# Layer 1's convolution stage as Strassen pairs on 128-token halves, with half of the weight sums on GpSimd

## The chip, the cores and the metric

The kernel runs on one core of a Trainium2 chip. The time is the device time of one execution in microseconds, the median of several runs; lower is better. Tiles have 128 partitions. The engines are TensorE (PE in the profile; its weight loads are PEld), VectorE (DVE), ScalarE (ACT), GpSimd (POOL) and SyncE (SP), which here only issues the weight transfers.

## The reference

Two transformer blocks in sequence, all in fp32, width 1024, on 256 tokens. The second has two layers and works on 256 context tokens beside the 256 latent ones. In its layer 0 both are carried through; in layer 1, the last, only the latent ones need the mixer's output. What matters here is the part of that mixer that the kernel calls the convolution stage:

```python
def _conv_module(glu, p):
    a, g = jnp.split(glu, 2, axis=-1)
    y = a * jax.nn.sigmoid(g)
    y = depthwise_conv_over_tokens(y, p['conv_w_dw'], width=31, pad=15) + p['conv_b_dw']
    y = silu(layernorm(y, p['conv_ln_g'], p['conv_ln_b']))
    return y @ p['w_conv_o']

def _merge(o_att, o_gla, r, glu, gates, p):
    y_att = o_att @ p['w_att_o']
    y_gla = (rmsnorm(o_gla) * silu(r)) @ p['w_gla_o']
    y_conv = _conv_module(glu, p)
    g_att, g_gla, g_conv = jnp.split(jax.nn.sigmoid(gates), 3, axis=-1)
    return (g_att * y_att + g_gla * y_gla + g_conv * y_conv) @ p['w_out']
```

`glu` (2048 columns) and `gates` (3072) are columns of `h @ w_in`. Each layer also needs a modulation vector `silu(c) @ w_ada + b_ada` of 6144 numbers for two conditions, which doesn't depend on the tokens. (The names are shortened from the reference.)

## The kernel before

Activations lie with features on partitions: `H`, `X`, `MX` are 8 chunks of 128 features by 512 tokens, the context in columns 0 to 255 (`CTX`), the latent tokens in 256 to 511 (`XS`). A weight tile is 128 output columns of a matrix, 512 KB, as 8 chunks of 128x128. SyncE streams the tiles in a fixed order into eight slots `W[0]` to `W[7]`; a slot's next load waits on the semaphore `unit`, which TensorE raises once for each tile, in order. The program is a list of stages; each engine runs its own instructions of every stage in a fixed order, and semaphores named by stage and turn tie the engines together. At the end of a stage each engine but SyncE and GpSimd raises `phase_done`; VectorE and ScalarE enter the next stage when all three have, and TensorE runs ahead where its semaphores allow.

*The convolution stage of layer 1* has eight turns, one for each 128 features of the output. A turn has six tiles in slots 0 to 5: the two halves of `glu` (value, gate), the gate of the attention branch, `w_att_o`, the gate of the recurrent branch (called gla), `w_gla_o`. TensorE's `conv` multiplies each by the 256 latent tokens (`project`, L613: eight products, each of which the profile shows as two instructions). ScalarE takes sigmoids. VectorE writes value times gate into `padded`, runs the 31 taps of the convolution as one instruction of 128x256 each on two accumulators in turn (L3609 to L3613), adds the accumulators and the running `tile_sum` for the coming norm (L3616, L3618), does one modulation tile and then gates the two branches into `MX` (L3626 to L3630).

*A modulation tile* (`ada_tile`, `ada_keep`; L2660, L2662, L2669) is a 128x1024 slice of `w_ada` times the two condition rows, summed on VectorE, and a small copy. There are 96 of them, spread over stages by the table `ADA_TURNS` as (turns, first buffer, tiles in a turn). GpSimd's queue loads them (`load_ada`), each when its buffer's last tile is done. Eight stand in layer 1's convolution stage ("conv1").

*Layer 0's convolution stage* is already written as Strassen-Winograd products (`conv_strassen`, `conv_begin`, `conv_middle`, `conv_end`). Two weight tiles A and B form a pair (attention gate with recurrent gate; glu's gate with glu's value). The input's feature chunks are split in even and odd, and the tokens in context and latent, 256 each. Seven products of half size take the place of eight: two with raw blocks (P1, P2), one each for sums of weights with sums of input blocks (V2, the cross product, V3), and two closing ones, one into the accumulator and one into the cross bank (`c12`). ScalarE copies the accumulator out between them (`held`), VectorE adds a copy and a bank for each of three results. Each pair needs four weight sums of 128x512: sums[0] = B even + B odd, sums[2] = A even + B even, sums[1] = sums[0] + A even, sums[3] = sums[1] + A odd; all are VectorE's. The four sums of input blocks (`sum_blocks`) are made once in a stage. TensorE's loop is rotated: close the first pair, open and mix and close the second, then open the next turn's first pair.

*The first merge stage* (`merge1`, 16 steps in the same manner, L841 and L891 on TensorE, L2673 and on in VectorE) has VectorE instructions of its own at 128x1024. *`conv_norm`* follows the convolution: TensorE computes two gate tiles, waits for all engines' end of the convolution stage, and then forms the mean from `tile_sum` (L1784). There GpSimd adds pairs of squares (`pair_squares`, L3785). *Layer 1's recurrent stage* (gla) comes before the convolution.

Of the kernel before, what the change touches and what calls it, by code (L numbers as in the profile page):

```python
# [19 lines left out]
ALU = mybir.AluOpType  # L20
# [3 lines left out]
P = 128  # L24
# [27 lines left out]
ADA_TURNS = {"out1": (2, 0, 4), "down1": (4, 0, 5), "attend": (3, 0, 4), "attend_last": (3, 0, 4), "up2": (10, 0, 2),  # L52
             "attend1": (2, 0, 4), "attend1_last": (2, 0, 4), "conv1": (8, 0, 1)}
# [16 lines left out]
def first_column(layer):  # L70

    return 0 if layer < LAYERS - 1 else S
# [136 lines left out]
def program(nc, params, consts, stream, ada, cond, x_in, mem_in, ctx_in, out, counted):  # L209
    plan = phases()  # L210
    with ExitStack() as ctx:
# [302 lines left out]
        def split(c0):  # L514
# [23 lines left out]
        H_SUMS, G_SUMS = 17, 17 + 4 + 2 * QUADS  # L538
# [4 lines left out]
                 for v in (SQF, WORK[:, 2048:6144])]  # L543
        q_parts = [[v[:, i * S:(i + 1) * S].rearrange("p (j t) -> p j t", j=2) for i in range(8)]
                   for v in (WORK[:, 0:2048], MXF[:, 2048:4096])]
        conv_even, conv_odd = ([YG[:, FT * T2 + (2 * i + p) * S:FT * T2 + (2 * i + p + 1) * S] for p in range(2)]
# [58 lines left out]
        def _(pe):  # L605
# [1084 lines left out]
            def conv(s):  # L1690

                cols = slice(first_column(s.layer), T2)
                n = T2 - cols.start
                pe.wait_ge(*s.before("glu"))
                for u in range(2):
                    project(s, u, bank[u][:, 0:n], cols)
                pe.wait_ge(*s.earlier("gla_end", 0))
                for b in range(2):
                    pe.wait_ge(*s.before(f"gate{b}"))
                    project(s, 2 + 2 * b, bank[2 + 2 * b][:, 0:n], cols)  # L1700
                    pe.wait_ge(*s.before(f"mixed{b}"))
                    project(s, 3 + 2 * b, bank[3 + 2 * b][:, 0:n], cols, src=Y2[b])
# [68 lines left out]
            def conv_norm_first(s):  # L1771
# [16 lines left out]
                for c in range(two, KC):  # L1788
                    if c >= 6:
# [7 lines left out]
                     "gla": (gla_begin, gla_middle, gla_end), "conv": conv, "merge2": merge2, ("merge2", 0): merge_strassen,  # L1797
# [10 lines left out]
        def _(act):  # L1808
# [539 lines left out]
            def conv(s):  # L2348
                n = T2 - first_column(s.layer)
                act.wait_ge(*s.done("unit", 1))  # L2350
                act.wait_ge(*s.before("glu"))
                act.activation(conv_sg[:, 0:n], bank[1][:, 0:n], ACT.Sigmoid).then_inc(*s.tick("glu_sig"))
                for b in range(2):
                    act.wait_ge(*s.done("unit", 2 + 2 * b))
                    act.wait_ge(*s.before(f"mixed{b}"))
                    act.activation(sg2[:, b, 0:n], bank[2 + 2 * b][:, 0:n], ACT.Sigmoid).then_inc(*s.tick(f"gate{b}"))
# [29 lines left out]
            def merge_strassen(s):  # L2386
# [23 lines left out]
                for p in range(1, 4):  # L2410
                    rest(p)
                    if p < 3:
# [5 lines left out]
                      "conv": conv, "conv_norm": conv_norm, "post_mixer": post_mixer, "ln_ffn": ln_ffn,  # L2418
# [12 lines left out]
        def _(dve):  # L2431
# [220 lines left out]
            def ada_tile(name, turn, k):  # L2652
# [3 lines left out]
                tile = (att_ada_w if name.startswith("attend") else ada_w)[u]  # L2656
                junk = att_ada_junk if name.startswith("attend") else {"up2": ada_w[5], "conv1": ada_w[4]}.get(name, ada_junk)
# [15 lines left out]
            def merge1(s):  # L2673
# [77 lines left out]
                for t in range(1, 16):  # L2751
# [839 lines left out]
            def conv(s):  # L3591
                c0 = first_column(s.layer)
                n = T2 - c0
                parts = slice(c0 // S, 2)
                dve.wait_ge(*s.done("glu_sig"))
                for at in (0, PAD + S):
                    link(s, dve.memset(padded[:, :, at:at + PAD], 0.0))
                dve.tensor_tensor(padded[:, parts, PAD:PAD + S], conv_sg[:, 0:n].rearrange("p (a t) -> p a t", t=S),
# [386 lines left out]
```

## Time and profile before

| | before |
|---|---|
| median of 3 runs | 3032.69 us (3031.74 to 3033.5) |
| the profiled execution, its own time | 3033.64 us |
| span from its first to its last instruction | 3031.8 us |
| TensorE busy | 2973.9 us, 98% |
| VectorE busy | 1909.4 us, 63% |
| ScalarE busy | 739.2 us, 24% |
| GpSimd busy | 62.8 us, 2% |

Busy times overlap, since the engines run side by side. Only time on the chain that ends last counts. The profiled execution is one run; its time stands 0.95 us above the median. Layer 1's convolution stage lies from about 2528 to 2695 us of the span, layer 0's from 1306 to 1611, the first merge stage from 436 to 631.

### The profile page before, as it was taken

Reading aid. Unit: us, or ns where it says so; the run is one execution under the profiler, and the core shown is the slowest. Engines: PE = TensorE matmul, PEld = TensorE weight load, DVE = VectorE, ACT = ScalarE, POOL = GpSimd, SP = SyncE. Lnnn points to the kernel's source line nnn. Section 1 sums busy time; section 2 is a strip of 40 time slices with the busy share of each in tenths; the row PEclk is TensorE's granted clock in tenths of the full one; section 3 lists DMA queues with packets and bytes.
Section 4 is the critical chain, followed back from the end, with each engine's and each line's share of the span. In section 5 each row is a group of like instructions: output and inputs, shape, how many; then the busy total and the mean of one; then the engine's idle time right before and its main releaser. Section 6 shows DMA issues by size and latency. Waiting matters only on the chain.

```text
span 3031.8 us, 45316 instructions
## 1 busy us (share of the span) xinstructions
PE 2973.9 (98%) x15958; PEld 2451.2 (81%) x15958; DVE 1909.4 (63%) x3765; ACT 739.2 (24%) x1786; POOL 62.8 (2%) x109
## 2 busy tenths in 40 slices
PE   9999999999999999999999999999999999999998
PEld 8888889989985566667775888888866778887998
DVE  4456326667656777768886566665357667863665
ACT  3334212212213333311113041110043431021111
POOL 0000000000010000000000000000000000000000
PEclk9999999999999999999999999999999999999999
DMA  5243334554562311112222114332223123434443
GB/s 194 93 149 111 139 125 168 170 208 163 198 227 104 127 53 50 63 63 83 83 83 89 63 49 146 125 125 90 90 92 119 65 86 129 176 132 153 153 150 115
DMA packets 105049, 363.97 MB, mean 120 GB/s; under 512 B 11488, under 2 KB 17632, under 8 KB 104800
## 3 DMA queue, kind: packets, MB, share of 16 engines
q1 hardware_dynamic: 90832, 310.94, 29.5%
q0 software_dynamic: 14096, 51.39, 4.8%
q8 instruction: 80, 1.31, 0.2%
q14 instruction: 41, 0.34, 0.0%
HBM read 361.23 MB, written 1.05 MB: 119 GB/s over the span
## 4 chain that ended last, share of the span: by engine, by line
PE 94%; DVE 3%; issue 1%; ACT 1%; DMA 1%; DVEq 0%; ACTq 0%; SPq 0%
PE bank L613 25%; PE bank L1126 7%; PE bank L1290 6%; PE bank L1708 5%; PE bank L841 5%; PE bank L1365 4%; PE bank L1592 4%; PE bank L1483 3%; PE bank L624 3%; PE bank L1606 2%; PE bank L1302 2%; PE bank L1456 2%; PE bank L1045 1%; PE bank L1651 1%; PE bank L1168 1%
## 5 line engine op out<-in xcount | busy, mean ns | idle before, releaser
L613 PE MATMUL bank<-H,W 128*128 128x256 f32 (+1 forms) x2048 | 497.3, 400 | 2.9 <-issue 2.8
L613 PEld LDWEIGHTS bank<-H,W 128*128 128x128 f32 x2048 | 386.9, 190 | 99.8 <-issue 52.0
L613 PE MATMUL bank<-YG,W 128*128 128x256 f32 (+1 forms) x912 | 258.9, 439 | 1.3 <-issue 0.8
L613 PEld LDWEIGHTS bank<-YG,W 128*128 128x128 f32 x912 | 172.9, 190 | 74.0 <-issue 56.6
L1483 PE MATMUL bank<-H,W 128*128 128x512 f32 (+1 forms) x320 | 119.4, 509 | 2.5 <-ACT H L2224 2.5
L1592 PE MATMUL bank<-W,H 128*128 128x256 f32 x512 | 118.8, 383 | 0.0
L1592 PEld LDWEIGHTS bank<-W,H 128*128 128x128 f32 x512 | 96.0, 193 | 13.8 <-issue 1.9
L1290 PE MATMUL bank<-MX,SQ 128*128 128x256 f32 x480 | 105.2, 379 | 0.0
L1290 PEld LDWEIGHTS bank<-MX,SQ 128*128 128x128 f32 x480 | 91.2, 190 | 12.4
L1483 PEld LDWEIGHTS bank<-H,W 128*128 128x128 f32 x320 | 58.8, 190 | 45.1 <-issue 38.2
L3655 DVE SCALAR_TENSOR_TENSOR YG<-WORK,PR,YG 128x512 f32 (+1 forms) x120 | 89.7, 747 | 0.0
L624 PEld LDWEIGHTS bank<-W,H 128*128 128x128 f32 x768 | 88.7, 192 | 0.8
L624 PE MATMUL bank<-W,H 128*128 128x128 f32 x768 | 89.0, 275 | 0.0
L1606 PE MATMUL bank<-H,W 128*128 128x512 f32 (+1 forms) x256 | 87.9, 486 | 0.0
L3655 DVE SCALAR_TENSOR_TENSOR WORK<-WORK,PR 128x512 f32<-128x512 f32 x112 | 83.7, 747 | 0.0
L1811 ACT ACT_TABLE_LOAD x21 | 26.9, 1283 | 213.7 <-DVEq L309 211.6
L1126 PE MATMUL bank<-H,W 128*128 128x128 f32 x640 | 77.7, 275 | 0.0
L1126 PEld LDWEIGHTS bank<-H,W 128*128 128x128 f32 x640 | 74.7, 192 | 0.1
L324 ACT ACTIVATE WORK<-bank,rowmax 128x128 f32<-128x128 f32 (+2 forms) x88 | 46.1, 530 | 117.3 <-DVE rowmax L317 117.3
L1708 PE MATMUL bank<-H,W 128*128 128x256 f32 x320 | 71.8, 379 | 0.3 <-issue 0.3
L1302 PE MATMUL bank<-H,W 128*128 128x256 f32 x320 | 70.8, 379 | 0.5 <-issue 0.5
L317 DVE TENSOR_REDUCE rowmax<-bank 128x1 f32<-128x128 f32 (+2 forms) x88 | 41.2, 494 | 46.0 <-PE bank L785 24.8
(633 smaller groups left out, 5841.8 us busy)
## 6 DMA issues: line engine op xcount, KB each, us to landing
W<-stream SPq DMA_DIRECT2D x556, 512.0 KB, 3.3
WORK<-ada POOLq DMA_DIRECT2D x44, 512.0 KB, 4.5
YG<-ada POOLq DMA_DIRECT2D x40, 512.0 KB, 3.6
W<-stream SPq DMA_DIRECT2D x24, 384.0 KB, 3.7
SQ<-ada POOLq DMA_DIRECT2D x12, 512.0 KB, 7.2
W<-stream SPq DMA_DIRECT2D x16, 128.0 KB, 2.3
CN<-consts SPq DMA_DIRECT2D x1, 1984.0 KB, 15.5
X<-x_in SPq DMA_DIRECT2D x2, 512.0 KB, 5.4
```

What stands on the lines that cost most here:

```text
L613: m = pe.matmul(out_ap, W[u][:, c, :], src[:, c, cols], start=first and c == 0, stop=last and c == k - 1)
L624: m = pe.matmul(o, H[:, c, col0 + t * P:col0 + (t + 1) * P], W[u][:, c, :], start=c == 0, stop=c == KC - 1)
L841: m = pe.matmul(out, w[:, c, :], b[:, c, :], start=first and c == 0, stop=c == KC // 2 - 1, skip_group_check=True)
L1126: m = pe.matmul(out, w[:, c, :], b[:, c, :], start=first and c == 0, stop=c == KC // 2 - 1, skip_group_check=True)
L1290: m = pe.matmul(out, w[:, c, :], b[:, c, :], start=first and c == 0, stop=c == KC // 2 - 1, skip_group_check=not first)
L1302: m = pe.matmul((acc, top)[c % 2][j], W[j][:, c, :], H[:, c, left], start=c < 2, stop=c >= KC - 2)
L1365: ends[q] = pe.matmul(out, w[q][:, c, :], b[:, 4 * q + c, :], start=first and q == 0 and c == 0, stop=q == 2 and c == n - 1, skip_group_ch ...
L1483: m = pe.matmul(out_bank[:, 0:T2 - cols.start], W[i][:, c, :], H[:, c, cols], start=c == 0, stop=c == KC - 1)
L1592: m = pe.matmul(o, H[:, c, t * P:(t + 1) * P], slots[:, 3:5, c, :], start=c == 0, stop=c == KC - 1)
L1606: m = pe.matmul(bank[6 + u][:, 0:n], W[5 + u][:, c, :], H[:, c, c0:T2], start=c == 0, stop=c == KC - 1)
L1708: m = pe.matmul(out, w[:, c, :], b[:, c, :], start=first and c == 0, stop=c == KC // 2 - 1, skip_group_check=not first)
L3655: o = dve.scalar_tensor_tensor(sums[tap % 2], src, w, sums[tap % 2], ALU.mult, ALU.add)
```

## The change

Layer 1's convolution stage takes the form of layer 0's. Since only the latent tokens are carried there, these are split in two halves of 128 (`left`, `right` on the input; `near`, `far` on the results) where layer 0 splits context from latent. The order of tiles in the stream becomes layer 0's. All seven products of a pair have 128 columns; the two mixes (`w_att_o`, `w_gla_o`) keep 256, and so do the taps. Of a pair's four weight sums, sums[1] and sums[3] are VectorE's and sums[0] and sums[2] are GpSimd's, in a loop of its own. The eight modulation tiles leave the stage; eight now stand in the first merge stage, after the even tile of steps 4, 5, 7, 8, 9, 11, 12 and 13, loaded into the first half of `cond_raw` in `MX`. In `conv_norm` nothing changes.

```diff
-ADA_TURNS = {"out1": (2, 0, 4), ..., "attend1_last": (2, 0, 4), "conv1": (8, 0, 1)}
+MERGE_ADA = (4, 5, 7, 8, 9, 11, 12, 13)
+ADA_TURNS = {"merge1": (8, 0, 1), "out1": (2, 0, 4), ..., "attend1_last": (2, 0, 4)}
...
+        late_t = [SQF[:, i * 512:(i + 1) * 512].rearrange("p (c t) -> p c t", c=KC // 2) for i in range(4)]
+        near, far = slice(0, P), slice(P, S)
...
@@ TensorE: conv is removed, conv_halves added @@
+                def open_pair(s, j, begins=False):
+                    acc, top, cross = (bank[5 - 3 * j + i][:, 0:P] for i in range(3))
+                    a, sums = W[3 * j], conv_w[j]
+                    pe.wait_ge(*s.before(f"acc_taken{j}"))
+                    pe.wait_ge(*s.done(f"loaded{3 * j}"))
+                    if begins:
+                        pe.wait_ge(*s.earlier("state1", 0))
+                    product(acc, a[:, EVEN, :], H[:, EVEN, left], first=True).then_inc(*s.tick(f"p1{j}"))
+                    if begins:
+                        pe.wait_ge(*s.earlier("scored", 0))
+                        pe.wait_ge(*s.before(f"mixed{j}"))
+                        project(s, 3 * j + 1, bank[j][:, 0:S], XS, src=Y2[j], tick=False)
...
+                    pe.wait_ge(*s.before(f"first_taken{j}"))
+                    product(top, a[:, ODD, :], H[:, ODD, left], first=True).then_inc(*s.tick(f"p2{j}"))
+                    pe.wait_ge(tally.sem("t_summed"), CONV_SUMS + 2)
+                    pe.wait_ge(*s.done(f"p1_held{j}"))
+                    pe.wait_ge(*s.done(f"w_summed{j}", 0))
+                    product(acc, sums[1], late_t[1]).then_inc(*s.tick(f"v2{j}"))
+                    pe.wait_ge(*s.before(f"cross_taken{j}"))
+                    pe.wait_ge(*s.done(f"w_summed{j}", 1))
+                    pe.wait_ge(*s.done("paired", 2 * j + 1))
+                    product(cross, sums[0], late_t[0], first=True).then_inc(*s.tick("unit"))
...
+                def close_pair(s, j):
+                    acc, cross = bank[5 - 3 * j][:, 0:P], bank[7 - 3 * j][:, 0:P]
+                    pe.wait_ge(tally.sem("t_summed"), CONV_SUMS + 4)
+                    pe.wait_ge(*s.done(f"v3_held{j}"))
+                    pe.wait_ge(*s.done(f"loaded{3 * j + 2}"))
+                    product(acc, W[3 * j + 2][:, ODD, :], late_t[3]).then_inc(*s.tick("unit"))
+                    pe.wait_ge(*s.done(f"corner_taken{j}"))
+                    product(cross, conv_w[j][3], H[:, ODD, right]).then_inc(*s.tick(f"c12{j}"))
...
@@ VectorE, first merge stage @@
+                    if t in MERGE_ADA:
+                        ada_tile("merge1", MERGE_ADA.index(t), 0)
+                        ada_keep("merge1", MERGE_ADA.index(t))
...
@@ VectorE: conv is removed @@
+            def late_sums(f, j):
+                a, sums, made = W[3 * j], conv_w[j], f"w_summed{j}"
+                dve.wait_ge(*f.done(f"loaded{3 * j}"))
+                dve.wait_ge(*f.done("paired", 2 * j))
+                dve.tensor_tensor(sums[1], sums[0], a[:, EVEN, :], ALU.add).then_inc(*f.tick(made))
+                dve.wait_ge(*f.done(made, 0))
+                dve.tensor_tensor(sums[3], sums[1], a[:, ODD, :], ALU.add).then_inc(*f.tick(made))
...
+            def late_begin(f):
...
+                late_sums(f, 0)
+                sum_blocks(late_t, tally.sem("t_summed"), CONV_SUMS, sides=(left, right))
+                dve.wait_ge(tally.sem("padding"), 4)
+                late_first(f, 0)
+                late_corner(f, 0)
+                late_sums(f, 1)
+                late_gate_cross(f)
+                late_mix_att(f)
+                late_first(f, 1)
+                late_corner(f, 1)
+                late_mix_gla(f)
+
+            def late_middle(s, f):
+                late_glu_left(s)
+                late_sums(f, 0)
+                late_glu_right(s)
+                late_taps(s, 0, 3)
+                late_first(f, 0)
+                late_taps(s, 3, 11)
+                late_corner(f, 0)
+                late_sums(f, 1)
+                late_taps(s, 11, 21)
+                late_gate_cross(f)
+                late_taps(s, 21, 23)
+                late_mix_att(f)
+                late_taps(s, 23, 25)
+                late_first(f, 1)
+                late_taps(s, 25, 29)
+                late_corner(f, 1)
+                late_taps(s, 29, CONV)
+                late_mix_gla(f)
+
+            def late_end(s):
+                late_glu_left(s)
+                late_glu_right(s)
+                late_taps(s, 0, CONV)
...
@@ GpSimd @@
+            def conv_weights():
+                where = next(n for n, (kind, l, _, _) in enumerate(plan) if (kind, l) == ("conv", 1))
+                pool.wait_ge(tally.sem("phase_done"), WORKERS * where)
+
+                def sums(f):
+                    for j in range(2):
+                        a, b, w = W[3 * j], W[3 * j + 2], conv_w[j]
+                        pool.wait_ge(*f.done(f"loaded{3 * j + 2}"))
+                        pool.wait_ge(*f.before(f"c12{j}"))
+                        pool.tensor_tensor(w[0], b[:, EVEN, :], b[:, ODD, :], ALU.add).then_inc(*f.tick("paired"))
+                        pool.wait_ge(*f.done(f"loaded{3 * j}"))
+                        pool.tensor_tensor(w[2], a[:, EVEN, :], b[:, EVEN, :], ALU.add).then_inc(*f.tick("paired"))
+
+                with pool.Fori(0, KC) as turn:
+                    sums(Step(tally, plan, where, turn))
+
+            pool.wait_ge(tally.sem("ada_done"), 1)
+            load_ada("merge1", 0, ("merge1", "out1"), cond_raw)
...
-            load_ada("ln_mixer", 1, ("attend1", "conv1"), att_ada_w)
-            load_ada("conv", 1, ("conv1", None), ada_w)
+            load_ada("ln_mixer", 1, ("attend1", None), att_ada_w)
+            conv_weights()
             pair_squares(1)
```

The functions `late_first`, `late_corner`, `late_gate_cross`, `late_mix_att`, `late_mix_gla`, `late_glu_left`, `late_glu_right` and ScalarE's `conv_halves` are layer 0's with these widths: `late_first`, `late_corner` and the cross additions read a held copy and a bank at 128x128, and the mixes a gate and a bank at 128x256.

## Rows read from the trace of the kernel before

**Rows 1.** Page, chain that ended last: share of the span by engine.

```profile
PE 94%; DVE 3%; issue 1%; ACT 1%; DMA 1%; DVEq 0%; ACTq 0%; SPq 0%
```

**Rows 2.** Windows, one turn: us, busy by engine, clock, DMA share, GB/s.

```profile
2549.10:2569.90 20.80, 20.80 (x98) 18.32 (x97) 17.57 (x45) 1.15 (x3) 0.53 (x1) 1.00 0.48 176
```

**Rows 3.** Chain in order of time: start us, us, engine, tile, line, instructions.

```profile
531.04 10.72 PE bank L841 x96
...
2528.37 166.02 PE bank L613 x768
```

**Rows 4.** Timeline, layer 1's last convolution turn: start us, us, engine, line, operation.

```profile
2682.16 0.41 DVE L3609 TENSOR_SCALAR YG<-WORK,PR 128x256 f32 x1 [0.31 <-DVE WORK L3598]
...
2682.75 0.48 DVE L3613 SCALAR_TENSOR_TENSOR YG<-WORK,PR,YG 128x256 f32 x1
...
2693.83 0.48 DVE L3613 SCALAR_TENSOR_TENSOR YG<-WORK,PR,YG 128x256 f32 x1
2694.35 0.42 DVE L3616 TENSOR_TENSOR YG<-YG,WORK 128x256 f32 x1
...
2695.47 1.23 DVE L2660 SCALAR_TENSOR_TENSOR WORK<-WORK,cond_row 128x1024 f32<-128x1024 f32 x1 [0.23 <-DVE tile_sum L3618]
...
2698.51 0.42 DVE L3626 TENSOR_TENSOR MX<-WORK,bank 128x256 f32 x1 [0.33 <-PE bank L613]
...
2699.58 0.42 DVE L3630 TENSOR_TENSOR MX<-MX,WORK 128x256 f32 x1
...
2701.51 0.59 PE L1784 MATMUL bank<-tile_sum,CN 128*128 128x256 f32 x2
```

**Rows 5.** Timeline, VectorE, one turn of layer 0's convolution stage.

```profile
1381.47 0.42 DVE L3666 SCALAR_TENSOR_TENSOR WORK<-WORK,bank 128x256 f32<-128x256 f32 x1 [0.22 <-PE bank L1708]
1381.87 0.69 DVE L3637 TENSOR_TENSOR W<-W 128x512 f32<-128x512 f32 x1
...
1384.41 0.41 DVE L3671 TENSOR_TENSOR WORK<-WORK,bank 128x256 f32<-128x256 f32 x1
...
1386.13 0.55 DVE L3651 TENSOR_SCALAR YG<-WORK,PR 128x512 f32 x1 [0.39 <-DVE WORK L3675]
...
1402.76 0.42 DVE L3694 TENSOR_TENSOR WORK<-WORK,bank 128x256 f32<-128x256 f32 x1
1403.09 0.75 DVE L3655 SCALAR_TENSOR_TENSOR WORK<-WORK,PR 128x512 f32<-128x512 f32 x1
1403.76 0.75 DVE L3655 SCALAR_TENSOR_TENSOR YG<-WORK,PR,YG 128x512 f32 x1
```

**Rows 6.** Page, DMA issues: line, count, KB, us to landing.

```profile
W<-stream SPq DMA_DIRECT2D x556, 512.0 KB, 3.3
```

**Rows 7.** Timeline, GpSimd's squares with VectorE beside them, layer 0, then layer 1.

```profile
1644.05 2.49 POOL L3785 TENSOR_TENSOR SQ<-SQ 128x512 f32<-128x512 f32 x2
1644.33 1.07 DVE L3378 TENSOR_TENSOR MOD<-MOD,PR 128x64 f32<-128x64 f32 x1
...
1645.43 1.14 DVE L3380 TENSOR_SCALAR MOD<-MOD 128x16 f32<-128x16 f32 x1
...
2704.87 0.22 DVE L3378 TENSOR_TENSOR MOD<-MOD,PR 128x64 f32<-128x64 f32 x1
```

**Rows 8.** Timeline, start of layer 1's convolution stage.

```profile
2529.87 0.69 DVE L3588 TENSOR_TENSOR YG<-WORK 128x512 f32 x1 [0.16 <-DVE WORK L3585]
...
2530.91 0.53 POOL L3776 DMA_DIRECT2D WORK<-ada  x1 [198.98 <-DVEq L309]
```

**Rows 9.** Timeline, end of layer 0's convolution stage.

```profile
1608.71 1.89 PE L1708 MATMUL bank<-H,WORK 128*128 128x256 f32 x8
...
1612.16 0.55 DVE L3651 TENSOR_SCALAR YG<-WORK,PR 128x512 f32<-128x512 f32 x1
```

**Rows 10.** Timeline, first merge stage, the gap on VectorE.

```profile
502.63 0.42 DVE L2742 TENSOR_TENSOR MX<-MX,WORK 128x256 f32<-128x256 f32 x1
...
506.48 0.42 DVE L2705 TENSOR_TENSOR WORK<-WORK,bank 128x256 f32<-128x256 f32 x1 [3.42 <-ACT WORK L2000]
```

More of the change, by code:

```diff
@@ L1688, in gla, with conv_halves, product, mix @@
                 m.then_inc(*s.tick("gla_out"))
[L1690 to L1702, printed above, removed]
+            def conv_halves():
+                def product(out, w, b, first=False):
+                    for c in range(KC // 2):
+                        m = pe.matmul(out, w[:, c, :], b[:, c, :], start=first and c == 0, stop=c == KC // 2 - 1,
+                                      skip_group_check=not first)
+                    return m
+                def open_pair(s, j, begins=False):
[10 more added lines that the diff above has]
+                        project(s, 3 * j + 1, bank[j][:, 0:S], XS, src=Y2[j], tick=False)
+                        pe.wait_ge(*s.earlier("r_taken", 0))
+                        pe.wait_ge(*s.earlier("head_rstd", 0))
+                    pe.wait_ge(*s.before(f"first_taken{j}"))
[8 more added lines that the diff above has]
+                    product(cross, sums[0], late_t[0], first=True).then_inc(*s.tick("unit"))
+                    pe.wait_ge(tally.sem("t_summed"), CONV_SUMS + 3)
+                    pe.wait_ge(*s.done(f"v2_held{j}"))
+                    for c in range(KC // 2):
+                        m = pe.matmul(acc, sums[2][:, c, :], late_t[2][:, c, :], start=False, stop=c == KC // 2 - 1,
+                                      skip_group_check=True)
+                        if begins and c == 0:
+                            m.then_inc(*s.tick("unit"))
+                    m.then_inc(*s.tick(f"v3{j}"))
+                def mix(s, j):
+                    pe.wait_ge(*s.before(f"mixed{j}"))
+                    project(s, 3 * j + 1, bank[j][:, 0:S], XS, src=Y2[j])
+                def close_pair(s, j):
[6 more added lines that the diff above has]
+                    product(cross, conv_w[j][3], H[:, ODD, right]).then_inc(*s.tick(f"c12{j}"))
+                def rest(s):
+                    close_pair(s, 0)
+                    open_pair(s, 1)
+                    mix(s, 1)
+                    close_pair(s, 1)
+                def middle(s, following):
+                    rest(s)
+                    open_pair(following, 0)
+                    mix(following, 0)
+                return lambda s: open_pair(s, 0, begins=True), middle, rest
@@ L3608, in conv @@
                     if tap == 0:
-                        o = dve.tensor_scalar(sums[0], src, w, par(f"conv_b{s.layer}", s.turn), ALU.mult, ALU.add)
+                        o = dve.tensor_scalar(sums[0], src, w, par("conv_b1", s.turn), ALU.mult, ALU.add)
                     elif tap == 1:
@@ L3861, in weight_stream @@
                 tiles += [unit(w, gate + n * D + i * P), unit(a[name][l], i * P)]
-            out += tiles if l else [tiles[n] for n in (2, 3, 4, 1, 5, 0)]
+            out += [tiles[n] for n in (2, 3, 4, 1, 5, 0)]
         out += [unit(w, gate + 2 * D + i * P) for i in range(8)]
```

134 lines of the change are left out of this document (86 added, 48 removed).

## The prediction, made before the changed kernel ran

> **What bounds the kernel now.** I read the page's chain of waits first: 94% of it is TensorE, 3% VectorE [rows 1]. A change gains only where it shortens TensorE's work or the few waits on others, and loses wherever it makes a new one. Then the busy times of one turn of the stage that changes: TensorE busy 20.80 of 20.80 us, VectorE 17.57, ScalarE 1.15, GpSimd 0.53, granted clock 1.00, the 2.4 GHz level [rows 2]. So the stage runs at TensorE's pace, with VectorE 3.2 us a turn below it. The chain in order of time gives TensorE's prices: the eight turns are one unbroken run of 768 instructions in 166.02 us, 216.2 ns for 256 columns; in the first merge stage 96 instructions of 128 columns take 10.72 us, 111.7 ns each [rows 3]. (An fp32 product appears as two instructions: 48 products of a turn are 96.) Two halves cost 223.4 ns against 216.2 ns for the whole, so halving is nearly free.
>
> **TensorE's sum.** Before, a turn is 96 x 216.2 ns = 20.75 us. After, each of two pairs has seven products of four blocks, 28 products, 56 instructions at 128 columns; both pairs 112 x 111.7 ns = 12.51 us. The two mixes stay: 32 x 216.2 ns = 6.92 us. Together 19.43 us: 1.32 us a turn, 10.6 us in eight. This is all that the change can give.
>
> **VectorE's sum.** It loses the modulation tile (from the tile-sum to the first mix, 2695.47 to 2698.51, 3.04 us) [rows 4]. It gains weight sums, held-plus-bank additions and four block sums at the stage's start. I price a turn of the new loop from two sources: the taps, which keep their 256 columns, from the old stage [rows 4], and the rest from layer 0's Strassen loop, same order at twice the columns [rows 5]. Its additions of 512 columns don't depend on token width. The elements that fall away go at the rate between layer 0's tap (1402.76 to 1403.09 is 0.33 us for 256 columns of an addition from a bank) and a quarter-size one; from taps, 0.66 us at 512 and 0.396 us at 256, that is 0.13 us for each 128 columns. So:
> - left glu: 0.40 - 0.13 = 0.27 us; right glu, two instructions and the ScalarE sigmoid between them, 1384.41 to 1386.13 = 1.72, less 0.28: 1.44 us [rows 5];
> - weight sums: layer 0 does four in 1381.87 to 1384.41, 2.54 us; two with the wait between them are 1.33 us, twice a turn 2.66 us [rows 5];
> - 31 taps from the first to the sum of the two accumulators 2682.16 to 2694.35 = 12.19 us, and the two closing additions to the next instruction 1.12 us [rows 4];
> - five additions of 128 columns from a bank, 0.33 - 0.13 = 0.20 each, 1.0 us; the first mix 0.33; the second mix, two dependent instructions, about 0.9 us [rows 5].
> Sum 19.9 us. With nothing else, VectorE and no longer TensorE (19.43) sets the turn, by 0.5 us.
>
> **GpSimd.** It gets four additions of 128x512 a turn. The only such additions before are its squares: two in 2.49 us, 1.24 us each [rows 7]; four are 5.0 us, well inside a turn. The weights are there in time: the last slot is reloaded when the second pair's first closing product is done; a load lands in 3.3 us [rows 6], and VectorE comes to that pair's sums 7.6 us later (0.27 + 1.33 + 1.44 + 11 taps of 0.396 + 0.4, less what two short first taps save). So by its own length GpSimd's work hides. But the rows show what it does to VectorE. While GpSimd adds from 1644.05, VectorE's 128x64 addition of two SBUF tiles starts at 1644.33 and takes 1.07 us, to 1645.40, where GpSimd's first of two ends (1645.29); the 128x16 tensor_scalar after it takes 1.14 us, to 1646.57, where the second ends (1646.54). In layer 1 the same 128x64 addition takes 0.22 us [rows 7]. VectorE stood still until GpSimd was through. The Trainium skill, "SBUF — State Buffer", section "Who interferes with whom", has this as a rule: a VectorE instruction with two SBUF inputs, or in a two-port mode, and a GpSimd instruction that reads SBUF exclude each other, whichever issued first holding the ports for its whole length. By the rule a VectorE instruction that came first pays nothing, which no row here shows.
>
> In the new loop 29 taps, four weight sums, the right glu, the closing additions and the last mix all read two SBUF tiles; about 16.5 of 19.9 us are exposed. Only additions from a bank and the gaps at the right glu are free. I bound what one GpSimd addition costs VectorE: below nothing (no exclusion); if GpSimd always slips in beside a free instruction or a gap, 1.24 less the 0.2 to 0.75 us of it, in all 3.3 us a turn; if it breaks in between taps, 1.24 and the 0.08 us by which taps overlap (0.48 long, 0.396 apart [rows 4]), 4 x 1.32 = 5.3 us. Two of the four become ready in the middle taps, two at the glu, so I take the middle, 4.3 us: **a turn of 24.2 us**. TensorE, with 19.43 us of work, then waits 4.8 us a turn, where the first weight sum of the next tile is late.
>
> **Start.** VectorE leaves the recurrence at 2530.56, GpSimd wakes at 2530.91 [rows 8]. GpSimd's first sum ends at 2532.15, VectorE needs it for its own; four GpSimd additions alternate with VectorE's two (0.6 and 0.7), to about 2537.3. Block sums follow, 0.6 each; the second is there at 2538.65. From there TensorE: three products 2.7, ScalarE's copy 0.4, two products 1.8, five of the other pair 4.45, mix 3.46, one product 0.9: 2552.4, VectorE's first left glu at 2552.5. Without exclusion the same walk gives 2548.8.
>
> **End.** Before, the glu products stood first in a turn, and the four others covered the taps; the mean product started at 2701.51, after two gate tiles, with VectorE done at 2700.00 [rows 4]. Now the glu pair's last product is the last of the turn, and all taps come after it. From layer 0's end: product over at 1610.60, first tap at 1612.16, 1.56 us [rows 9]; at half width 1.2. VectorE then needs 0.27 + 1.2 + 12.19 + 0.9 us = 14.6 us from its last left glu; TensorE has only two gate tiles, 6.9 us, and then stands about 7.5 us. Even if turns ran at TensorE's pace, three quarters of the saving would be given back here.
>
> **Merge stage.** The moved tile is 3.04 us on VectorE, in eight turns. VectorE idles there from 503.06 to 506.48, 3.42 us [rows 10], and the tile stands in that gap. It costs nothing; if it came 1 us later each time, it would delay an addition that TensorE needs only about 4 us later, so the upper bound stays near nothing too. The eight GpSimd DMAs there are one more transfer of 512 KB to a turn's four; loads are issued a turn ahead. The queues behind (next stage's tiles) still start at their own stage. After the mean product nothing changes.
>
> **The sum.** Mean product at 2552.5 + 7 x 24.2 + 14.65 = 2736.5; before 2701.51; +35.0 us. The profiled execution took 3033.64 us (span 3031.8, 1.8 around it), 0.95 above the median 3032.69. 3033.64 + 35.0 = 3068.6; against the median 3067.7: I say 3068. By lower and upper cost per turn (23.2, 25.2): 3061 and 3075. Strided weight tiles may cost GpSimd more than contiguous squares; at 1.5 us instead of 1.24, 7 x 4 x 0.26 = 7 us more.
>
> **Rivals.**
> - *No exclusion, VectorE bound.* 2548.8 + 7 x 19.9 + 14.65 = 2702.75, +1.2 us: 3034, no change. For it: GpSimd's work is short and off the chain. Against: [rows 7]. It decides when GpSimd's additions cost VectorE under about 0.1 us each. Chance 0.11.
> - *The saving arrives.* If the turn is TensorE's 19.43 and the tail hides, 10.6 us less, 3022; it needs VectorE's end within 6.9 us of the last product, against 14.3 above. Chance 0.04.
> - *GpSimd starved.* Back-to-back taps keep GpSimd out until VectorE itself waits for its sum. Then each addition costs its whole 1.24 and TensorE's wait for the next sum comes on top, a turn of 26 us and more: 3068 + 7 x 1.8 = 3080 and above. For it: the taps leave no gap. Against: layer 0's two engines alternated. Chance 0.05.
>
> My forecast has 0.80, of which a little lies below 3042, where half of the additions would find free places.
>
> **How the numbers follow.** 0.2%, 6 us, is what a measurement here can tell. Slower 0.80 + 0.05, same 0.11, faster 0.04. Range 3042 to 3080: forecast with its bounds.
>
> **What the profile after would show.** Right: taps that last 1.5 us and more instead of 0.48, one to four a turn, each next to a GpSimd addition; TensorE idle 4 to 5 us a turn, released by VectorE's weight sum; period 23 to 25.5 us; TensorE idle some 7.5 us before the mean product. Wrong: all taps 0.48 and a period under 20.5 (no exclusion); GpSimd additions much longer than 1.3 us (starved, or strided tiles dearer); in the merge stage, TensorE waits where there were none; a granted clock below 1.00 while TensorE waits, which would lengthen its own 19.43.

## The result, and the profile after

The changed kernel takes 3084.61 us (median of 4 runs, 3078.98 to 3087.81), before 3033.1 us in the same comparison; the ratio is 1.0168 (95% interval 1.0151 to 1.0186). Slower, as predicted, but 16.6 us above the 3068 us that I gave and 4.6 us above the end of the range. The profiled execution took 3082.31 us (span 3080.5), 48.7 us above the profiled one of before; the steps below are counted against that. I had 35.0. The four executions come in the order of their granted clock: 3078.98 us at 0.994, 3082.31 at 0.993, 3086.9 at 0.992, 3087.81 at 0.991.

The page of the changed kernel, chain of waits, shares of the span (against [rows 1]):

```profile
PE 89%; DVE 5%; issue 3%; ACT 1%; DVEq 0%; DMA 0%; POOL 0%; ACTq 0%; SPq 0%; POOLq 0%
```

TensorE loses 5 points of the chain. The windows of four turns of the stage, each from one left glu (L3699) to the next, columns as in [rows 2]:

```profile
2552.36:2577.73 25.37, 22.18 (x150) 20.72 (x149) 22.44 (x49) 3.16 (x12) 5.74 (x4) 0.93 0.37 126
2653.67:2680.88 27.21, 23.26 (x146) 21.41 (x145) 22.41 (x49) 3.16 (x12) 5.74 (x4) 0.87 0.34 114
2680.88:2708.14 27.26, 23.23 (x146) 21.35 (x145) 22.40 (x49) 3.16 (x12) 5.88 (x4) 0.87 0.33 117
2708.14:2732.75 24.61, 21.45 (x144) 20.18 (x143) 20.64 (x48) 3.16 (x12) 2.97 (x2) 0.93 0.36 128
```

These are turns 1, 5, 6 and 7; turns 2 to 4 took 25.31, 25.33 and 25.30 us. The seven make 180.39 us, 25.77 each, where I had 24.2. No engine is busy throughout: VectorE, which I had as the bound, works 22.4 of 25.4 us. And the granted clock, 1.00 in the turn of [rows 2], is under it in turns 1, 3, 5, 6 and 7 (0.93, 0.93, 0.87, 0.87, 0.93); in turns 2 and 4 it is 1.00.

Turn 1 in the timeline, VectorE and GpSimd, the first pair of additions and the second:

```profile
2557.19 0.48 DVE L3689 SCALAR_TENSOR_TENSOR WORK<-WORK,PR 128x256 f32<-128x256 f32 x1
2557.33 1.46 POOL L3949 TENSOR_TENSOR WORK<-W 128x512 f32<-128x512 f32 x1 [8.58 <-DMA W<-stream]
2557.58 1.49 DVE L3689 SCALAR_TENSOR_TENSOR YG<-WORK,PR,YG 128x256 f32 x1
2558.75 1.45 POOL L3951 TENSOR_TENSOR WORK<-W 128x512 f32<-128x512 f32 x1
2558.99 1.48 DVE L3689 SCALAR_TENSOR_TENSOR WORK<-WORK,PR 128x256 f32<-128x256 f32 x1
...
2567.70 1.49 DVE L3689 SCALAR_TENSOR_TENSOR YG<-WORK,PR,YG 128x256 f32 x1
2568.87 1.45 POOL L3951 TENSOR_TENSOR W<-W 128x512 f32<-128x512 f32 x1
2569.11 0.41 DVE L3733 TENSOR_TENSOR MX<-WORK,bank 128x256 f32 x1
2569.44 1.16 DVE L3689 SCALAR_TENSOR_TENSOR WORK<-WORK,PR 128x256 f32<-128x256 f32 x1
```

The exclusion is there as forecast: a tap that meets a GpSimd addition lasts 1.49 us instead of 0.48 and ends 0.3 us after it. Three taps lose 1.01 us each; the fourth addition falls partly over the mix from a bank (L3733, 0.41 us as ever) and costs 0.69. Together 3.73 us a turn. GpSimd pays too: 1.45 us an addition, 1.26 at the stage's start where VectorE waits for it.

What I had not forecast stands between those rows. The same turn, ScalarE with TensorE and VectorE around it (in brackets the idle time before, and its releaser):

```profile
2562.72 0.28 ACT L2412 ACTIVATE WORK<-bank 128x128 f32<-128x128 f32 x1 [0.52 <-PE bank L1699]
...
2567.11 0.28 DVE L3727 TENSOR_TENSOR WORK<-WORK,bank 128x128 f32<-128x128 f32 x1
...
2567.42 0.31 ACT L2412 ACTIVATE WORK<-WORK 128x128 f32<-128x128 f32 x1 [4.42 <-DVE WORK L3727]
...
2567.64 0.26 ACT L2409 ACTIVATE WORK<-bank 128x128 f32<-128x128 f32 x1
...
2568.14 3.50 PE L1699 MATMUL bank<-SQ,WORK 128*128 128x128 f32 x16 [2.85 <-ACT WORK L2409]
...
2571.23 0.31 ACT L2412 ACTIVATE WORK<-WORK 128x128 f32<-128x128 f32 x1 [3.33 <-DVE WORK L3716]
2571.44 0.26 ACT L2409 ACTIVATE WORK<-bank 128x128 f32<-128x128 f32 x1
...
2571.85 1.13 PE L1730 MATMUL bank<-SQ,WORK 128*128 128x128 f32 x8 [0.20 <-ACT WORK L2409]
...
2573.39 0.29 DVE L3722 TENSOR_TENSOR WORK<-WORK,bank 128x128 f32<-128x128 f32 x1 [0.62 <-ACT WORK L2409]
...
2576.64 0.42 DVE L3739 TENSOR_TENSOR WORK<-WORK,bank 128x256 f32<-128x256 f32 x1 [1.23 <-PE bank L618]
```

Read it from the end. VectorE waits 1.23 us for the second mix (L618) and 0.62 us for a copy. Those are late because TensorE began the glu pair's V2 (and the cross product behind it, 16 instructions together) only at 2568.14, after 2.85 us idle, released by ScalarE's copy of the pair's first product (L2409, 2567.64). That product had long been done. But ScalarE's queue is in order, and in front of the copy stands the gates pair's far sigmoid (L2412, 2567.42), which waits for VectorE's cross addition (L3727, 2567.11), placed after 21 taps. So TensorE's path hangs on VectorE's place in the taps, through a ScalarE queue in which both stand. The next copy is caught in the same way behind the near sigmoid (2571.23), which waits for VectorE at 2570.92. With 0.20 us ahead of the left glu, for which the view names no releaser, this makes 2.05 us a turn in which VectorE, the bound of my sum, waits; 1.85 of them for the engine that waits for it. So TensorE's idle time is released by ScalarE's copies, and in none of the seven turns by VectorE's weight sum, as I had it: in turn 2, at full clock, 0.51, 2.82 and 1.66 us, together the 4 to 5 us that I forecast.

Turn 5, one of the two long ones:

```profile
2669.41 3.06 PE L1699 MATMUL bank<-SQ,WORK 128*128 128x128 f32 x16 [2.81 <-ACT WORK L2409]
...
2673.12 2.05 PE L1730 MATMUL bank<-SQ,WORK 128*128 128x128 f32 x8 [0.65 <-ACT WORK L2409]
2674.96 4.65 PE L618 MATMUL bank<-YG,W 128*128 128x256 f32 x16
...
2675.58 0.29 DVE L3722 TENSOR_TENSOR WORK<-WORK,bank 128x128 f32<-128x128 f32 x1 [1.53 <-ACT WORK L2409]
...
2679.82 0.42 DVE L3739 TENSOR_TENSOR WORK<-WORK,bank 128x256 f32<-128x256 f32 x1 [2.22 <-PE bank L618]
```

V3 takes 2.05 us where it takes 1.13 at full clock, and the mix 4.65 where it takes 3.62: the granted clock is 0.50 over V3, the lower of the two levels (1.2 GHz), and 0.78 over the mix. VectorE's two waits grow from 1.85 to 3.75 us, which is the turn's 1.9 us.

The stage's start:

```profile
2528.74 1.26 POOL L3949 TENSOR_TENSOR W<-W 128x512 f32<-128x512 f32 x1 [197.55 <-DVEq L310]
...
2530.10 1.68 DVE L3674 TENSOR_TENSOR W<-W 128x512 f32<-128x512 f32 x1 [1.50 <-POOL W L3949]
...
2531.20 1.71 POOL L3949 TENSOR_TENSOR WORK<-W 128x512 f32<-128x512 f32 x1
2531.82 1.63 DVE L3676 TENSOR_TENSOR W<-W 128x512 f32<-128x512 f32 x1
2532.86 1.70 POOL L3951 TENSOR_TENSOR WORK<-W 128x512 f32<-128x512 f32 x1
2533.37 1.74 DVE L3225 TENSOR_TENSOR SQ<-H 128x512 f32<-128x512 f32 x1
...
2535.89 3.78 PE L1699 MATMUL bank<-SQ,W 128*128 128x128 f32 x16 [4.46 <-DVE SQ L3227]
```

The engines alternate as predicted. Each instruction now lasts 1.6 to 1.7 us instead of 0.6 and 1.24, but these spans overlap, each with the other engine's turn in it, so the whole is no longer than in my walk. TensorE's 16 instructions behind it (V2 and the cross product) take 3.78 us instead of 2.05, at a granted clock of 0.50, after 4.46 us idle. And the end (against [rows 4]):

```profile
2747.36 0.43 DVE L3694 TENSOR_TENSOR tile_sum<-tile_sum,YG 128x256 f32<-128x256 f32 x1
...
2747.90 1.22 PE L1842 MATMUL bank<-tile_sum,CN 128*128 128x256 f32 x2 [7.11 <-DVEq L310]
2748.92 5.21 PE L618 MATMUL bank<-H,W 128*128 128x256 f32 x16
```

The mean product comes after 7.11 us of idle, as forecast (7.5), takes 1.22 us instead of 0.59 [rows 4], and the gate tiles after it 5.21 us where 3.62 is usual.

### The profile page after: what moved, and what is told of

Its sections match the earlier page's. It is cut to its first block, busy times and chain, and to the rows that moved or that the text cites. A ratio compares the mean times of both kernels' runs of the same rounds, so it can differ in the third digit from the quotient of the medians.

```text
span 3080.5 us, 46472 instructions
## 1 busy us (share of the span) xinstructions
PE 2983.2 (97%) x16342; PEld 2467.5 (80%) x16342; DVE 1969.0 (64%) x3843; ACT 756.1 (25%) x1858; POOL 110.3 (4%) x141
## 3 DMA queue, kind: packets, MB, share of 16 engines
HBM read 361.23 MB, written 1.05 MB: 118 GB/s over the span
## 4 chain that ended last, share of the span: by engine, by line
PE 89%; DVE 5%; issue 3%; ACT 1%; DVEq 0%; DMA 0%; POOL 0%; ACTq 0%; SPq 0%; POOLq 0%
PE bank L618 20%; PE bank L1131 7%; PE bank L1295 6%; PE bank L1766 5%; PE bank L846 5%; PE bank L1370 4%; PE bank L1597 3%; PE bank L1488 3%; PE bank L629 3%; PE bank L1611 2%; PE bank L1307 2%; PE bank L1461 2%; PE bank L1050 1%; PE bank L1656 1%; PE bank L1173 1%
## 5 line engine op out<-in xcount | busy, mean ns | idle before, releaser
L618 PE MATMUL bank<-H,W 128*128 128x256 f32 (+1 forms) x1536 | 385.6, 408 | 2.5 <-issue 2.3
L618 PEld LDWEIGHTS bank<-H,W 128*128 128x128 f32 x1536 | 290.8, 191 | 86.3 <-issue 51.0
L618 PE MATMUL bank<-YG,W 128*128 128x256 f32 (+1 forms) x912 | 261.1, 442 | 0.9 <-issue 0.8
L618 PEld LDWEIGHTS bank<-YG,W 128*128 128x128 f32 x912 | 173.6, 192 | 73.3 <-issue 56.0
L1488 PEld LDWEIGHTS bank<-H,W 128*128 128x128 f32 x320 | 58.8, 190 | 45.2 <-issue 38.2
L1869 ACT ACT_TABLE_LOAD x21 | 26.9, 1283 | 218.3 <-DVEq L310 216.2
L1131 PEld LDWEIGHTS bank<-H,W 128*128 128x128 f32 x640 | 74.7, 192 | 0.1
```

The source lines that it names most:

```text
L618: m = pe.matmul(out_ap, W[u][:, c, :], src[:, c, cols], start=first and c == 0, stop=last and c == k - 1)
L1131: m = pe.matmul(out, w[:, c, :], b[:, c, :], start=first and c == 0, stop=c == KC // 2 - 1, skip_group_check=True)
L1488: m = pe.matmul(out_bank[:, 0:T2 - cols.start], W[i][:, c, :], H[:, c, cols], start=c == 0, stop=c == KC - 1)
```

## The experiments

Seven kernels take the change apart, and three are built on what these showed. Times are medians; ratios are to the kernel before, with 95% intervals. e1 to e6 keep the change and edit it at one place or two.

**e1: GpSimd's additions taken out.** sums[0] and sums[2] are then stale, so this kernel leaves out half of the weight sums.

```diff
-  pool.tensor_tensor(w[0], b[:, EVEN, :], b[:, ODD, :], ALU.add).then_inc(...)
+  pool.nop().then_inc(...)
-  pool.tensor_tensor(w[2], a[:, EVEN, :], b[:, EVEN, :], ALU.add).then_inc(...)
+  pool.nop().then_inc(...)
```

> GpSimd's four weight additions of each turn are left out; its semaphore ticks stay, so sums[0] and sums[2] are stale. Measured turn of the changed kernel at full clock: 25.33 us. Theory A (exclusion, and a second bound: ScalarE's copy of the second pair's first product stands in its queue behind a sigmoid that waits for VectorE's first cross addition, so TensorE's second half of a turn starts only there): only the two additions ahead of that cross addition are on the path, 2 x 1.01 us; turn 23.3 us, some 4 us less at the start, total about 3065 us. Theory B (exclusion and VectorE's own length alone, as predicted): turn 19.9 us, total about 3040 us. Theory C (no exclusion, the long taps have another cause): 3084 us, unchanged.

Measured 3046.42 us, ratio 1.005 (1.0033 to 1.0066). Windows, turn 1:

```profile
2546.32:2567.91 21.59, 20.58 (x149) 19.18 (x148) 18.72 (x49) 3.16 (x12) 0.00 (x0) 1.00 0.43 148
```

25.33 to 21.59 (21.58 or 21.59 in turns 2 to 6) is 3.74 us, the 3.73 read off the four stretched instructions: every one lay on the path. So both theories missed: A let only two of the four count (23.3 us), B had no wait for TensorE (19.9); C is out. The first left glu comes 6.0 us sooner, where A had 4. The clock is 1.00 in all seven turns. VectorE's waits of 1.24, 0.61 and 0.20 us stay, so they are no child of the exclusion. In this kernel TensorE idles 0.87 us ahead of the glu pair's V2 in turn 1, not 2.85.

**e2: ScalarE's order.** The glu pair's first and second copy go ahead of the sigmoids that wait for VectorE. Nothing else. (In short: each call stands for its waits and its one instruction.)

```diff
+  early(1, late_glu_held)        # copy of the first product
+  second(1, late_glu_held)       # copy of V2
   far_sig(0, late_gate)          # waits for VectorE's cross addition
-  early(1, late_glu_held)
   near_sig(1, late_glu)
-  second(1, late_glu_held)
   third(1, late_glu_held)
```

> All work kept; only ScalarE's order changes: the second pair's first and second copies come ahead of the first pair's last sigmoid. Theory A: VectorE's waits for TensorE go (2.05 us a turn), VectorE then sets the turn with 19.6 + 3.7 us of exclusion, 23.3 to 23.5 us; total about 3069 us. Theory B: ScalarE's order is not on the path, 3084 us, unchanged.

Measured 3070.75 us, ratio 1.0127 (1.011 to 1.0144): 14 us back by the medians, 9.6 us between the profiled executions (3072.69 against 3082.31). Turns now 23.71, 26.02, 26.19, 24.12, 24.24, 23.86, 22.05. From the timeline of turn 1:

```profile
2565.73 1.95 PE L1699 MATMUL bank<-SQ,WORK 128*128 128x128 f32 x16
...
2575.60 0.42 DVE L3757 TENSOR_TENSOR WORK<-WORK,bank 128x256 f32<-128x256 f32 x1 [0.30 <-DVE tile_sum L3712]
```

V2 starts at once, and VectorE's wait for the mix is gone. Turn 1 is 1.7 us shorter. Turns 4 to 6, at clock 1.00, are 1.1 to 1.5 us shorter and miss the 23.3 to 23.5 of theory A: in turns 4 and 5 VectorE now waits 0.73 us ahead of the first mix, for ScalarE's far sigmoid, and 0.30 ahead of the second. The clock still falls, to 0.87 in turns 2 and 3 and to 0.95 over 2550:2680: TensorE's idle time has moved, not vanished, since VectorE at 23.7 us is still far above TensorE's work.

**e3: both.** Stale weight sums again, and the new order.

> Both edits: ScalarE's new order, and GpSimd's additions left out (sums[0] and sums[2] stale). Theory A: the turn is VectorE's own sum or TensorE's, 19.5 to 20.0 us, granted clock back at 1.00; the mean product then still waits some 7 us for the last turn's taps; total about 3038 us. Theory B: the same as without the additions alone.

Measured 3041.71 us, ratio 1.003 (1.0018 to 1.0041). Turns 1 to 6 take 20.74 to 20.77 us, by chance TensorE's old turn; theory A had at most 20.0.

```profile
2562.41 0.42 DVE L3751 TENSOR_TENSOR MX<-WORK,bank 128x256 f32 x1 [0.69 <-ACT WORK L2412]
```

Of the 1.85 us that the order frees, 0.69 come back as this new wait (the first mix for the far sigmoid, now two places later in ScalarE's queue) and 0.30 as the second mix's wait for the instruction before it. So with two of four weight sums free and no exclusion at all, the two-pair form is still 9.7 us slower than before (3032.02 in the same comparison): start, VectorE's own work and the tail are enough.

**e4: each GpSimd addition twice,** the first time into an unused tile.

```diff
+  pool.tensor_tensor(MX[:, 4 * j:4 * j + 4, 0:P], b[:, EVEN, :], b[:, ODD, :], ALU.add)
   pool.tensor_tensor(w[0], b[:, EVEN, :], b[:, ODD, :], ALU.add).then_inc(...)
+  pool.tensor_tensor(MX[:, 4 * j:4 * j + 4, P:S], a[:, EVEN, :], b[:, EVEN, :], ALU.add)
   pool.tensor_tensor(w[2], a[:, EVEN, :], b[:, EVEN, :], ALU.add).then_inc(...)
```

> Each of GpSimd's four additions is done twice a turn, the first time into a part of MX that nothing reads; the rest is the changed kernel. Theory A: each addition ahead of the first cross addition stops one tap for 1.01 us: two more there are 2.0 us a turn; the two more behind it fall mostly into VectorE's waits for TensorE (2.05 us): turn 27.4 us, total about 3099 us. Exclusion without that slack: 4.0 us a turn, about 3113 us. No exclusion: 3084 us.

Measured 3117.96 us, ratio 1.0283 (1.0266 to 1.03). The timeline has the pattern of the changed kernel, twice as long:

```profile
2592.97 1.44 POOL L3950 TENSOR_TENSOR WORK<-W 128x512 f32<-128x512 f32 x1
2593.21 1.48 DVE L3689 SCALAR_TENSOR_TENSOR YG<-WORK,PR,YG 128x256 f32 x1
2594.38 1.44 POOL L3952 TENSOR_TENSOR MX<-W 128x512 f32<-128x512 f32 x1
2594.62 1.49 DVE L3689 SCALAR_TENSOR_TENSOR WORK<-WORK,PR 128x256 f32<-128x256 f32 x1
```

Turns 1 to 6 take 30.5 to 32.1 us, 5.2 to 6.8 more for four further additions, 1.3 to 1.7 each, and the time is 5 us above the dearest of the theories. In turn 2 the eight stretched instructions lose 7.8 us against 3.73, so 1.0 for each further addition; the other 1.4 us are longer waits for TensorE, at a granted clock of 0.89. So this run confirms the mechanism, but its size per addition is not a clean price.

**e5: all weight sums on VectorE,** as layer 0 has them; GpSimd's loop is gone.

```diff
+  dve.tensor_tensor(sums[0], b[:, EVEN, :], b[:, ODD, :], ALU.add).then_inc(*f.tick(made))
+  dve.tensor_tensor(sums[2], a[:, EVEN, :], b[:, EVEN, :], ALU.add).then_inc(*f.tick(made))
...
   dve.tensor_tensor(sums[1], sums[0], a[:, EVEN, :], ALU.add).then_inc(*f.tick(made))
...
```

> The changed kernel with all four weight sums of a pair on VectorE, none on GpSimd. With GpSimd's additions left out a turn took 21.59 us. The four sums that come back cost VectorE 0.6 us each, 2.4 us. Theory A (exclusion, each GpSimd addition stops VectorE for 0.7 to 1.0 us): turn 24.0 us against 25.3, no dip of the granted clock, the start some 3 us shorter; total about 3065 us, 20 us less than with GpSimd. Theory B (work off VectorE is worth having, the exclusion is small beside it): more VectorE work makes it slower than the changed kernel, over 3085 us.

Measured 3067.53 us, ratio 1.0111 (1.0095 to 1.0126). The windows of two turns:

```profile
2548.89:2573.01 24.12, 20.66 (x150) 19.26 (x149) 21.19 (x54) 3.15 (x12) 0.00 (x0) 1.00 0.40 132
2646.60:2670.65 24.05, 20.30 (x146) 18.89 (x145) 21.14 (x52) 3.15 (x12) 0.00 (x0) 1.00 0.38 131
```

17 us faster than with GpSimd's help (14 between the profiled executions). The turn is theory A's 24.0; turn 3 alone took 25.49 us at a granted clock of 0.93, a dip that the theory had excluded. Four additions on VectorE cost 24.05 - 21.59 = 2.46 us a turn; on GpSimd they cost it 3.74.

**e6: other banks for the gate tiles of `conv_norm`,** so that TensorE does more of them before the mean product.

```diff
-  one, two = (2, 3) if s.layer else (4, 5)
+  one, two = (5, 6) if s.layer else (4, 5)
```

(and, in layer 1, waits before each gate tile for the bank's last reader.)

> The changed kernel, but in layer 1's norm TensorE computes five gate tiles ahead of the mean product and one behind it, not two and one. The wait of 7.1 us ahead of the mean product should go. If nothing is given back, 3077.5 us. If the three tiles that used to cover the norm's chain behind the mean are missed there (10.4 us of them), up to all of it is given back: 3077 to 3085 us.

Measured 3079.87 us, ratio 1.0153 (1.0137 to 1.0168); 4.7 us below the changed kernel's median, which is not clear of noise: the intervals overlap, and the profiled executions are 2.0 us apart. Timeline, then TensorE's waits after it:

```profile
2751.50 0.59 PE L1843 MATMUL bank<-tile_sum,CN 128*128 128x256 f32 x2
```

```profile
PE bank L618 <- ACT WORK L2289: 3.6, 1, 3.6
```

No idle time ahead of the mean, and 0.59 us for it: the 1.22 belongs to the 7 us of idle. But 3.6 us of the 7.1 come back as a wait for ScalarE within the next 50 us.

**e7: the kernel before with only the modulation tiles moved.**

> The kernel before with one part of the change alone: its eight modulation tiles move from layer 1's convolution stage to the first merge stage. VectorE had 3.4 us of idle time a step there and TensorE's waits in the merge stage did not change in the changed kernel. Expected: the same as before, 3032 us, within 1.5 us. If the moved tiles delayed the merge stage, up to 8 x 1 us more there.

Measured 3033.12 us (11 runs) against 3033.38 (21 runs), ratio 0.9998 (0.9989 to 1.0007). The mean product stands at 2700.35, 1.2 us before that of [rows 4]. Moving the tiles costs and brings nothing that can be measured, as the prediction had it.

**e8: one pair.** From here on a repair is tried. What TensorE saves has to be bought with VectorE's time: in [rows 2] VectorE has 3.2 us a turn to spare, two pairs need more, one may not. Only the two gates are a Strassen pair on halves, all its weight sums are VectorE's; glu's two tiles are plain 256-column products again and stand first in the turn, so that the end of the stage is the old one.

```diff
+  for u in range(2):
+      project(s, u, bank[u][:, 0:S], XS)              # glu, plain
...
+      product(acc, sums[2], late_t[2]).then_inc(*s.tick("v30"))
...
+      project(s, 3, bank[2][:, 0:S], XS, src=Y2[0])   # first mix
```

> Only the pair of gates as Strassen products on the halves; glu's two tiles stay plain and first in a turn; all four weight sums of that pair on VectorE; modulation tiles in the merge stage; stream order as before. TensorE: 48 x 216.2 ns for the four plain tiles and 56 x 111.7 ns... that is 64 instructions at 216.2 (13.84 us) and 56 at 111.7 ns (6.26 us), 20.1 us a turn, 0.66 us less than before. VectorE: 19.5 less the glu pair's additions, about 18.5 us a turn. If TensorE sets the turn: 8 x 0.66 = 5.3 us less, about 3027 us. If the queues' order makes waits as in the changed kernel, more than 3032 us.

Measured 3028.83 us (11 runs) against 3033.38 (21 runs), ratio 0.9987 (0.9978 to 0.9996). Windows, one turn:

```profile
2549.55:2569.89 20.34, 20.31 (x122) 18.50 (x121) 17.71 (x46) 2.31 (x8) 0.00 (x0) 1.00 0.47 155
```

TensorE is busy throughout again and VectorE has room. The turn, 20.33 us from first tap to first tap, is 0.24 us above the 20.09 that 56 x 111.7 + 64 x 216.2 ns [rows 3] give.

**e9: the lesson of e2 in e8.** ScalarE's copy of V2 goes ahead of the near sigmoid.

```diff
+  hold(0, "v2", late_gate_held[:, 1, :])
   act.wait_ge(*s.done("first_taken0"))
   sigmoid(late_gate[:, near], "gate_sig0")
-  hold(0, "v2", late_gate_held[:, 1, :])
...
```

> e8 with ScalarE's copy of the gates pair's second left product put ahead of its sigmoid over the near half; nothing else. Theory (in e8 the copy stands behind a sigmoid that waits for VectorE, and TensorE's third product waits 0.24 us for it in each of the eight turns): the turn falls from 20.33 to about 20.1 us, the time from 3028.8 to about 3027. Rival (the 0.24 us are the copy's own length after the second product, whatever stands before it): turn 20.33, time 3029.

Measured 3026.05 us (11 runs, 3025.74 to 3028.17) against 3033.49 (21 runs), ratio 0.9979 (0.997 to 0.9988).

```profile
2549.57:2569.64 20.07, 20.07 (x122) 18.42 (x121) 17.71 (x45) 2.41 (x8) 0.00 (x0) 1.00 0.44 157
```

The turn is 20.07 us, the theory's 20.1, and this version beats both kernels.

**e10: e9 with two of the four weight sums on GpSimd,** the changed kernel's split.

> e9 with the weight sums 0 and 2 of its one pair on GpSimd, as in the changed kernel, and the other two on VectorE. Each GpSimd addition costs VectorE about 1.0 us beside it and saves VectorE about 0.6 us of its own. Theory (TensorE sets this turn and VectorE has about 1.5 us to spare in it): the 0.8 us more per turn fall into the spare time and the time is that of e9, within 2 us. Rival (the additions fall beside the work that TensorE waits for): up to 2 x 1.0 us in each of eight turns, 6 to 16 us above e9.

Measured 3027.41 us (11 runs), ratio 0.998 (0.9971 to 0.9989): that of e9. From the timeline of a turn:

```profile
2587.48 1.83 POOL L3878 TENSOR_TENSOR W<-W 128x512 f32<-128x512 f32 x1 [17.09 <-DMA W<-stream]
...
2588.21 1.38 DVE L3668 TENSOR_TENSOR YG<-YG,WORK 128x256 f32 x1
2589.27 1.45 POOL L3880 TENSOR_TENSOR W<-W 128x512 f32<-128x512 f32 x1
2589.62 1.37 DVE L3669 TENSOR_TENSOR tile_sum<-tile_sum,YG 128x256 f32<-128x256 f32 x1
```

The two closing additions of the turn last 1.38 us instead of 0.43, stretched as the taps are in the changed kernel. The turn stays at 20.07 us: here VectorE has the time, and the same exclusion costs nothing that can be measured; nor does taking two sums off VectorE gain anything.

## Why the prediction was wrong in its size

Of the 48.7 us between the profiled executions I had 35.0. By the steps of the prediction:

- **TensorE's sum and VectorE's own work: right.** VectorE's own work was 25.33 - 3.73 - 2.05 = 19.55 us, predicted 19.9. The 111.7 and 216.2 ns gave e9's turn to 0.02 us.
- **The exclusion: the mechanism right, its size 3.73 us a turn against 4.3.** The bounds were 3.3 and 5.3. My 1.24 + 0.08 for a break between taps was too dear: a tap loses 1.01. e1 removes it to the hundredth, e5 turns it round. The rival *no exclusion* is out.
- **"Turn of 24.2 us": the step that failed.** I added VectorE's work and the exclusion and let VectorE never wait. It waits 2.05 us a turn, most of it because ScalarE's copies for TensorE stand behind sigmoids that wait for VectorE. The order was in the diff and in ScalarE's code; I priced ScalarE only where the glu and the start pass through it. e2 shows it: with the copies first, turn 1 is 1.7 us shorter, the turns at full clock 1.1 to 1.5, and the time 13.9 us lower. It can't show the whole 2.05, since the same edit makes new waits of 0.73 and 0.30 us. Turns without a clock dip would then have been 4.3 - 3.73 = 0.6 us cheaper than I said for the exclusion, 0.35 for the work, and 2.05 dearer: 25.3.
- **The clock: named as a way to be wrong, not priced.** Turns 5 and 6 are 1.9 us longer each, and in turn 7 VectorE's waits are 3.1 us instead of 2.05. In e1 and e3, where TensorE idles under 1 us at a time in the turns, the clock is 1.00 in all of them.
- Seven turns: 180.39 against 169.4, +11.0. It is made of +14.35 (7 x 2.05), -4.0 (7 x 0.57), -2.45 (7 x 0.35), +3.8 (clock in turns 5 and 6), and -0.7 for the last turn, where GpSimd has only two additions: that spares VectorE 1.8 us, and the lower clock takes 1.05 of them back.
- **Start: 25.8 us from the recurrence's last pair of instructions to the first left glu (2526.60 to 2552.36) against 23.7 in my walk (2528.84 to 2552.5), +2.1.** The alternation of GpSimd and VectorE was right: TensorE's V2 comes 9.29 us after that pair, in the walk 9.81. What I had wrong is full clock after the wait: TensorE's three products behind it take 5.13 us (2535.89 to 2541.02, granted clock 0.55) instead of 2.7. The other 0.2 lie in the products after them. That the glu came at the predicted 2552.4 is luck: the stage began 2.24 us earlier.
- **Tail: 15.15 us against 14.65, +0.5;** TensorE's idle time 7.11 against 7.5. After the mean product +2.3, of which the rows show 0.63 for the product itself and 1.6 for the gate tiles behind it.
- **Moved tiles: nothing, right;** e7.
- Before the stage -2.24, which I had as nothing. About 1.7 of it lie at 2366 us in the execution of before, where sixteen instructions of TensorE took 5.31 us at a granted clock of 0.67; after, the same sixteen took 3.62. It is not the change's: e3's execution has the same 5.31. The other 0.5 is open.

Sum: 35.0 + 11.0 + 2.1 + 0.5 + 2.3 - 2.24 = 48.7. The rival *GpSimd starved* named 3080 and more, which is where the time fell, but not for its reason: in the rows of the turns GpSimd gets in within 0.36 us of the 1.26 it takes alone (1.62 is the longest of the 26 additions). What stays open: why the clock dips in turns 1, 3, 5 and 6 and not in 2 and 4, when all have the same 2.8 us of idle, and why only in some it falls late enough to reach VectorE; whether a GpSimd instruction that only writes SBUF would leave VectorE alone, which was not tried; and why e8, e9 and the changed kernel reach the stage 1.1 to 1.2 us before e7, which keeps the old one. About 1.2 of the 7.4 us by which e9 beats the kernel before are of this kind; 8 x 0.66 = 5.3 us are its turns; 0.9 are not accounted for.

## What to carry to other kernels

Before a wait is called hidden, write out the in-order queue of the helper engine as well: a copy that frees the critical engine must not stand behind an instruction that waits for a third one; two copies moved up were worth 10 to 14 us here, and one, in another form, 3. A second engine is no help to VectorE where each of its instructions stops VectorE for 1.0 us and spares it 0.6; it is harmless only where VectorE has that much to spare. And where a cheaper product is bought with another engine's time, buy as much as that engine has left: one pair gains 0.2%, two pairs lose 1.7%.

## What the runs showed of the hardware

- A GpSimd addition of 128x512 costs VectorE 1.01 us when it comes between back-to-back taps (1.49 instead of 0.48), and itself lasts 1.27 to 1.62 us in the changed kernel's turns (mostly 1.45) instead of 1.26, 1.7 when VectorE's instructions are of 512 columns too, and up to 2.00 in e10. A VectorE addition from a bank of 128x256 beside it keeps its 0.41 us. An instruction with a single tile as input isn't spared: in e2's turn 4 the two `tensor_scalar` that open the taps last 0.95 and 1.35 us beside GpSimd instead of 0.41 and 0.35. The Trainium skill, "SBUF — State Buffer", section "Who interferes with whom", says that of the two the instruction that issued first holds the ports for its whole length. The rows agree on who goes first: the tap that runs when the addition comes (2557.19) keeps its 0.48 us, and the addition grows by 0.20 us, of the 0.34 that this tap had left; the next tap lasts until 0.3 us past the addition's end. The start in the timeline doesn't always tell the order, though: in e10 a tap that starts at 2587.69, after the addition (2587.48, 1.83 us), still takes 0.49 us.
- TensorE's idle gaps can have a price beyond their length. After gaps of 3.82 us (e2, turn 2), 4.46 (the changed kernel's start) and 6.24 to 7.25 us (e4's turns) the next sixteen instructions of 128 columns took 3.77 or 3.78 us instead of 2.05, and the mean product after 7.1 us takes 1.22 instead of 0.59 in all of e1 to e5. After shorter gaps it differs between equal turns: in the changed kernel 3.50 us after 2.85 in turn 1, but 2.05 after 2.82 in turn 2, and in e5 2.05 in turns 2, 4, 5 and 6 and 2.52 in turn 3, all after 1.99 us. Turn 2 of the changed kernel:

```profile
2593.48 2.05 PE L1699 MATMUL bank<-SQ,WORK 128*128 128x128 f32 x16 [2.82 <-ACT WORK L2409]
```

So the length of the gap alone doesn't decide, and what does isn't shown. In turns 1 and 3 the slower instructions ran beside VectorE's longer path and cost nothing; in turns 5, 6 and 7 they reached the path.
